# Two thirds of each feed-forward output projection as seven block products in place of eight

## The reference, cut to what matters

```python
def half_swiglu(x, g, w_in, w_out):
    a, b = jnp.split(rms_norm(x, g) @ w_in, 2, axis=-1)
    return x + 0.5 * ((jax.nn.silu(a) * b) @ w_out)
```

## Time and profile before

| | us |
|---|---|
| median of 3 runs (2575.33 to 2577.39) | 2577.12 |
| span of the profiled execution, first to last instruction | 2573.1 |
| TensorE busy in it | 2505.8 |
| VectorE / ScalarE / GpSimd busy in it | 1650.9 / 1284.6 / 805.2 |

### The profile page before, as it was taken

One profiled execution on the slowest core, in us unless ns is written; L12 is line 12 of the kernel. 1 busy time (PEld: TensorE's weight loads), 2 busy tenths in 40 slices (PEclk: granted clock), 3 DMA queues, 4 the chain that ended last, 5 costly groups with the idle time before them and its releaser, 6 DMA issues.

```text
span 2573.1 us, 48280 instructions
## 1 busy us (share of the span) xinstructions
PE 2505.8 (97%) x19339; PEld 2434.2 (95%) x19339; DVE 1650.9 (64%) x2629; ACT 1284.6 (50%) x2161; POOL 805.2 (31%) x618
## 2 busy tenths in 40 slices
PE   8999999899999989999999999999999997999998
PEld 8999999799999979999999999999998986999998
DVE  8733856888888878743766852864345548871764
ACT  7633742455555557643755742753233327661652
POOL 2232233444444442232232233233222221223222
PEclk9999999899999999999999999999999999999999
DMA  7734632133333326644635743643434333653652
GB/s 201 170 107 119 166 97 86 51 102 101 101 101 101 101 71 166 160 118 116 159 109 139 167 123 105 167 117 134 151 101 135 121 104 89 158 143 102 152 137 78
DMA packets 93305, 316.70 MB, mean 123 GB/s; under 512 B 12288, under 2 KB 16000, under 8 KB 78784
## 3 DMA queue, kind: packets, MB, share of 16 engines
q1 hardware_dynamic: 53952, 242.78, 27.8%
q0 software_dynamic: 39168, 71.32, 16.5%
HBM read 223.44 MB, written 19.32 MB: 94 GB/s over the span
## 4 chain that ended last, share of the span: by engine, by line
PE 92%; DVE 4%; DMA 2%; ACT 1%; issue 1%; POOL 0%; SPq 0%; DVEq 0%; ACTq 0%; POOLq 0%
PE ps L1415 11%; PE ps L1423 11%; PE ps L1417 11%; PE ps L1440 7%; PE ps L1441 7%; PE ps L1447 7%; PE ps L1343 7%; PE ps L1344 6%; PE ps L1349 6%; PE ps L1724 1%; DMA sb_lw<-sb_rawf 1%; PE ps L1725 1%; PE ps L1726 1%; PE ps L1388 1%; PE ps L1380 1%; PE ps L1381 1%
## 5 line engine op out<-in xcount | busy, mean ns | idle before, releaser
L1417 PE MATMUL ps<-sb_ual,sb_hw 128*128 128x288 f32 x2240 | 617.4, 296 | 0.0
L1415 PE MATMUL ps<-sb_uah,sb_hw 128*128 128x288 f32 x2240 | 615.3, 298 | 0.0
L686 POOL DMA_DIRECT2D sb_lw<-sb_rawf x240 | 207.1, 864 | 710.2 <-ACT sb_lw L850 691.1
L1415 PEld LDWEIGHTS ps<-sb_uah,sb_hw 128*128 128x128 f32 x2240 | 423.1, 189 | 0.2 <-issue 0.2
L1417 PEld LDWEIGHTS ps<-sb_ual,sb_hw 128*128 128x128 f32 x2240 | 421.6, 188 | 0.0
L662 POOL TENSOR_TENSOR sb_wl<-sb_raw,sb_wh 128x1024 fp32r<-128x1024 f32 (+1 forms) x106 | 261.1, 2466 | 433.7 <-ACT sb_wh L813 416.9
L1423 PE MATMUL ps<-sb_uah,sb_lw 128*128 128x288 f32 x2240 | 389.0, 296 | 6.1 <-DMA sb_lw<-sb_rawf 6.1
L1343 PE MATMUL ps<-sb_uh,sb_wh 128*128 128x256 f32 (+1 forms) x1360 | 373.9, 303 | 6.6 <-DVE sb_zs L2338 3.2
L1441 PE MATMUL ps<-sb_hl,sb_hw 128*128 128x288 f32 x1388 | 374.0, 296 | 0.0
L1440 PE MATMUL ps<-sb_hh,sb_hw 128*128 128x288 f32 x1388 | 373.7, 297 | 0.0
L1344 PE MATMUL ps<-sb_ul,sb_wh 128*128 128x256 f32 (+1 forms) x1360 | 368.1, 297 | 0.0
(11 more groups left out here) (319 smaller groups left out, 4785.0 us busy)
## 6 DMA issues: line engine op xcount, KB each, us to landing
sb_rawf<-w_ffn_in SPq DMA_DIRECT2D x87, 1024.0 KB, 5.0
sb_lw<-sb_rawf POOLq DMA_DIRECT2D x272, 256.0 KB, 3.7
sb_raw<-w_ssd SPq DMA_DIRECT2D x64, 512.0 KB, 3.7
sb_rawf<-w_ffn_out SPq DMA_DIRECT2D x32, 768.0 KB, 4.2
sb_rawf<-w_ffn_out SPq DMA_DIRECT2D x32, 640.0 KB, 3.9
sb_raw<-w_att SPq DMA_DIRECT2D x40, 512.0 KB, 3.6
sb_h<-state SPq DMA_DIRECT2D x8, 1024.0 KB, 4.9
ssm_sample<-sb_h SPq DMA_DIRECT2D x8, 1024.0 KB, 4.7
```

Source lines behind the costliest of these rows:

```text
L686: pool.dma_start(slot(lw, p), rawf[:, s % 2, i * BL:(i + 1) * BL], accum_op=ALU.add).then_inc(ld_in[i], 16)
L1415: pe.matmul(out, w[:, k * P:(k + 1) * P], uah[:, SIDE[p], k, :], start=begins and k == 0, stop=False, skip_group_check=True)
L1417: pe.matmul(out, w[:, k * P:(k + 1) * P], ual[:, SIDE[p], k, :], start=False, stop=False, skip_group_check=True)
```

## The change

The units of an FFN are numbered anew, 30 in place of 22 inner tiles with two rounds of eight outputs. After inner tiles 0 to 7 (units 0 to 7) come four output units over these eight tiles: unit 8 is plain and does output tiles 0 and 1 (`plain_out`, two parts); units 9, 10 and 11 do the pairs of output tiles (2,3), (4,5) and (6,7) by the seven products of `times`, now with h as the activation side. Tiles 8 to 15 and units 20 to 23 do the same again. Tiles 16 to 21 (units 24 to 29) then go through eight plain units `out(f, m)` as before, but 6 tiles deep (KO); the first two of these are interleaved in `first_outs`.

For the seven products h needs sums over pairs of inner tiles and token halves. VectorE makes them (`h_side3`, `h_sides`, `h_side4`), ScalarE their high parts (`high_hs`, `high_h4`), VectorE their low parts (`low_hs`, `low_h4`). The results of the products are added to x one by one by VectorE (`add_product`, 288 tokens each) as they stand in PSUM, since the later products go on accumulating in the same bank; TensorE waits on the semaphore x_part for that. The weights of these units are loaded as 1 MB blocks from a new array w_ffn_so, and handled as those of an inner tile. `gate` and `up` no longer exist: gr and hr, seven slots of 288 for each of four pairs of tiles, lie at the addresses of hh and hl, and all is made in place; pc keeps one slot. So `low_h` of a tile comes one unit later than before in the first 16 tiles, after the side sums that read hr. Weights of the outputs that remain use three regions of hw and lw in place of two. The distance of silu and hidden to the products of their tile, and the scaling of gate and up by rms, are as before.

The new order and the new functions (other engines' waits, semaphore names, addresses and the host's layout of the weights are left out):

```diff
+FIRST, SECOND = "first", "second"
+FULL = 2
+PLAIN_OUT = (8, 20)
+PLAIN = (0, 1) + PLAIN_OUT
+FAST_OUT = (9, 10, 11, 21, 22, 23)
+INNER = tuple(i for i in range(NU) if i not in PLAIN_OUT + FAST_OUT)
+FAST = tuple(i for i in range(NU) if i not in PLAIN)
+LAST_PART = 24
...
+REGION = (0, 1, 2, 0, 1, 2, 0, 2)
+KO = 6
...
+        for i in range(NU):
+            u = f * NU + i
+            if i < FULL:
+                yield from ((u, FIRST), (u, SECOND))
+            elif i in PLAIN_OUT:
+                yield from ((u - 1, 4), (u, FIRST), (u, SECOND))
+            elif i == FULL:
+                yield from ((u, p) for p in (1, 5, 6, 2, 3, 7))
+            elif i - 1 in PLAIN_OUT:
+                yield from ((u, p) for p in (1, 2, 5, 6, 3, 7))
+            else:
+                yield from ((u, 1), (u, 5), (u - 1, 4), (u, 6), (u, 2), (u, 3), (u, 7))
+        yield u, 4
...
+            def plain_out(s):
+                f, n, q = s // NU, s % NU, nth_full(s)
+                c = PLAIN_OUT.index(n)
+                before = nth_tile(s - 1)
+                def highs(part, ms):
+                    b = bank_full(s, part)
+                    for m in ms:
+                        if m < 2:
+                            pe.wait_ge(hp_done, 4 * q + 2 * part + m + 1)
+                        at = place(s, 2 * part + m % 2) + m // 2 * P
+                        w = hw[:, at:at + P]
+                        for h, a in enumerate(PARTS[part][m % 2][1:]):
+                            pe.matmul(ps[:, b + h, 0:HALF], w, hh[:, m // 2, a, :], start=m == 0, stop=False)
+                            pe.matmul(ps[:, b + h, 0:HALF], w, hl[:, m // 2, a, :], start=False, stop=False)
+                def lows(part, ms):
+                    b = bank_full(s, part)
+                    for m in ms:
+                        if m < 2:
+                            pe.wait_ge(lp_in[2 * part + m], 16 * (q + 1))
+                        at = place(s, 2 * part + m % 2) + m // 2 * P
+                        w = lw[:, at:at + P]
+                        for h, a in enumerate(PARTS[part][m % 2][1:]):
+                            ins = pe.matmul(ps[:, b + h, 0:HALF], w, hh[:, m // 2, a, :], start=False, stop=m == KD - 1)
+                pe.wait_ge(gate_scaled, nth_tile(s - 2) + 1)
+                pe.wait_ge(h0_free, 2 * nth_in(s - 2) + 2)
+                pe.wait_ge(h_ready, before - 1)
+                highs(0, range(4))
+                times(s - 1, 4)
+                highs(0, range(4, 6))
+                lows(0, range(6))
+                pe.wait_ge(h0_free, 2 * nth_in(s - 1 if c == 0 else s - 2) + 1)
+                highs(1, range(6))
+                lows(1, range(6))
+                pe.wait_ge(h_ready, before + 1)
+                for part in range(2):
+                    highs(part, range(6, KD))
+                    lows(part, range(6, KD)).then_inc(prod_done, 1)
...
+            def first_outs(f):
+                u, s = U_FFN[f], f * NU + NU - 1
+                before = nth_tile(s)
+                pe.wait_ge(gate_scaled, before)
+                pe.wait_ge(h0_free, 2 * nth_in(s))
+                pe.wait_ge(h_ready, before - 3)
+                pe.wait_ge(wh_done, u + 1)
+                out_highs(f, 0, range(2))
+                times(s, 4)
+                pe.wait_ge(h_ready, before)
+                out_highs(f, 0, range(2, 5))
+                pe.wait_ge(wl_done, u + 1)
+                out_lows(f, 0, range(5))
+                pe.wait_ge(h0_free, 2 * nth_in(s) - 1)
+                pe.wait_ge(wh_done, u + 2)
+                out_highs(f, 1, range(5))
+                pe.wait_ge(wl_done, u + 2)
+                out_lows(f, 1, range(5))
+                pe.wait_ge(h_ready, before + 1)
+                for m in range(2):
+                    out_highs(f, m, range(5, KO))
+                    out_lows(f, m, range(5, KO)).then_inc(unit_done, 1)
...
+            def add_direct(s, p):
+                i = BLOCK[p]
+                pool.wait_ge(nd_done, nth_direct(s, p))
+                pool.dma_start(slot(lw, p), rawf[:, s % 2, i * BL:(i + 1) * BL], accum_op=ALU.add).then_inc(ld_in[i], 16)
...
+                for n in range(NU):
+                    s = f * NU + n
+                    if n < FULL:
+                        for i in range(4):
+                            add_full(s, i)
+                    elif n in PLAIN_OUT:
+                        add_full(s, 0)
+                        add_full(s, 1)
+                        add_full(s, 2)
+                        add_direct(s + 1, 1)
+                        add_full(s, 3)
+                    elif n - 1 in PLAIN_OUT:
...
+            def high_hs(f, c, j):
+                act.wait_ge(hs_made, 3 * nth_pair(f, c, j) + 3)
+                nc.scalar.copy(hh[:, j, S1:S4, :], hr[:, j, S1:S4, :]).then_inc(hs_high, 1)
+            def high_h4(f, c):
+                act.wait_ge(h4_made, nth_pair(f, c, 3) + 1)
+                act.wait_ge(prod_done, DONE[f * NU + PLAIN_OUT[c], SECOND])
+                nc.scalar.copy(hh[:, :, S4, :], s4r[:, :, :]).then_inc(hs_high, 1)
...
+            def plain_out(s):
+                f, c = s // NU, PLAIN_OUT.index(s % NU)
+                high_full(s, 2)
+                direct(s + 1, 1)
+                high_full(s, 3)
+                silu(s - 1)
+                high_h(s - 1)
+                direct(s + 1, 2)
+                direct(s + 1, 3)
+                high_hs(f, c, 3)
+                high12(s + 1)
+            def fast_out(s):
+                f, n = s // NU, s % NU
+                if n - 1 in PLAIN_OUT:
+                    high_h4(f, PLAIN_OUT.index(n - 1))
+                    high34(s)
+                    direct(s + 1, 1)
+                    direct(s + 1, 2)
+                    high12(s + 1)
+                    direct(s + 1, 3)
+                else:
+                    direct(s + 1, 1)
+                    high34(s)
+                    high12(s + 1)
+                    direct(s + 1, 2)
+                    direct(s + 1, 3)
...
+            def h_side3(f, c, j):
+                dve.wait_ge(h_made, TILES * f + 8 * c + 2 * j + 1)
+                V.tensor_tensor(hr[:, j, S3, :], hr[:, j, A21, :], hr[:, j, A11, :], ALU.subtract).then_inc(hs_made, 1)
+            def h_sides(f, c, j):
+                dve.wait_ge(h_made, TILES * f + 8 * c + 2 * j + 2)
+                dve.wait_ge(hs_made, 3 * nth_pair(f, c, j) + 1)
+                V.tensor_tensor(hr[:, j, S2, :], hr[:, j, A22, :], hr[:, j, S3, :], ALU.add).then_inc(hs_made, 1)
+                V.tensor_tensor(hr[:, j, S1, :], hr[:, j, A22, :], hr[:, j, A21, :], ALU.add).then_inc(hs_made, 1)
+            def h_side4(f, c, j):
+                dve.wait_ge(hs_made, 3 * nth_pair(f, c, j) + 2)
+                V.tensor_tensor(s4r[:, j, :], hr[:, j, A12, :], hr[:, j, S2, :], ALU.subtract).then_inc(h4_made, 1)
+            def low_hs(f, c, j):
+                dve.wait_ge(hs_high, nth_side(f, c, j) + 1)
+                dve.wait_ge(h4_made, nth_pair(f, c, j) + 1)
+                V.tensor_tensor(hl[:, j, S1:S4, :], hr[:, j, S1:S4, :], hh[:, j, S1:S4, :].bitcast(F32),
+                                ALU.subtract).then_inc(hs_ready, 1)
+            def low_h4(f, c):
+                dve.wait_ge(hs_high, nth_side(f, c, 4) + 1)
+                V.tensor_tensor(hl[:, :, S4, :], s4r[:, :, :], hh[:, :, S4, :].bitcast(F32), ALU.subtract).then_inc(hs_ready, 1)
+            def add_plain(s, part):
+                f, b = s // NU, bank_full(s, part)
+                key = (FIRST, SECOND)[part]
+                dve.wait_ge(prod_done, DONE[s, key])
+                if s % NU != PLAIN_OUT[0]:
+                    dve.wait_ge(x_part, UPDATED[s - PLAIN_OUT[1] + PLAIN_OUT[0], key])
+                V.scalar_tensor_tensor(two(x[:, part, :]), ps[:, b:b + 2, 0:HALF], 0.5, two(x[:, part, :]),
+                                       ALU.mult, ALU.add).then_inc(x_part, 1)
+            def add_product(s, p):
+                f, n, a = s // NU, s % NU, bank_a(s)
+                m, half = ((pair_tiles(s)[0], 0) if p in (1, 2) else (pair_tiles(s)[0], 1) if p == 4
+                           else (pair_tiles(s)[1], 0) if p in (6, 3) else (pair_tiles(s)[1], 1))
+                earlier = {2: 1, 3: 6, 7: 5}
+                dve.wait_ge(prod_done, DONE[s, p])
+                if p in earlier:
+                    dve.wait_ge(x_part, UPDATED[s, earlier[p]])
+                elif n > PLAIN_OUT[1]:
+                    dve.wait_ge(x_part, UPDATED[s - PLAIN_OUT[1] + PLAIN_OUT[0], {1: 2, 5: 7, 6: 3, 4: 4}[p]])
+                t0, w = HALVES[half]
+                bank = a + {2: 2, 3: 1, 5: 1}.get(p, 0)
+                V.scalar_tensor_tensor(x[:, m, t0:t0 + w], ps[:, bank, 0:w], 0.5, x[:, m, t0:t0 + w],
+                                       ALU.mult, ALU.add).then_inc(x_part, 1)
+                s = f * NU
...
+                    if n in (5, 7, 17, 19):
+                        low_hs(f, c, int(n in (7, 19)))
```

(67 more changed lines are left out.)

892 lines of the change are left out of this document (487 added, 405 removed).

## The result

The changed kernel takes **2542.24 us** (median; 2540.4 to 2547.8), the kernel before 2577.26 beside it: ratio 0.9868, 95% interval 0.9853 to 0.9883. Predicted were 2545.0, 2538 to 2560.

What follows compares the result with a forecast made beforehand. TensorE was taken as the bound, an FFN lasting as long as its matmuls. Terms: -38.3 + 1 + 3.5 + 1.5 + 0.3 = -32.0 us, so 2577.1 becomes 2545.1; range 2538 to 2560.

Steps and rivals of the forecast that it cites:

- Matmuls: All four FFNs: 984 output matmuls each in place of 1056, 288 fewer at 0.133 us, 38.3 us gained.
- VectorE in inner tiles: Inner tiles: VectorE's added sums and low parts of h fit its 1.82 us wait per tile; cost zero.
- Fast units: Fast output units: VectorE's seven adds and the low parts come in time; cost zero, thinnest cover 0.5 us.
- Rival 3: Fast output units: products wait for in-order adds to leave their bank; decides from 1.6 us per unit, up to 2596; chance 0.04.
- Plain units: Plain output units: block 3's transfer may land late, 0 to 2.5 us for each of 8; taken 0.1 each, 1 us.
- FFN 1 to 2: Handover from FFN 1 to FFN 2: TensorE waits for late block copies and the last block; 3.5 us, bounds 0 and 6.
- FFN 2 to attention: End of FFN 2: output 7's add 0 to 3 us late, next projection has no slack; 1.5 us.
- The end: Last output: second token half has 18 matmuls, not 30, to cover the first half's norm; 0.3 us, bounds 0 and 1.6.
- Rival 4: Products with h as moving side don't come at 133 ns; 2016 matmuls x 5 ns, 10 us, giving 2555; chance 0.04.

Runs made afterwards that it cites:

- count_back: Changed kernel with 288 matmuls put back as repeats, 12 in each of the 24 fast output units: 2572.43 us (0.998).
- before_less: Kernel before with 288 low-weight output matmuls left out and nothing else changed: 2536.64 us (0.9838).
- probe_large: Changed kernel with an unneeded VectorE reciprocal, about 1.25 us, ahead of product 6's add in 16 steady fast output units: 2556.5 us (0.9927).
- load_later: Changed kernel with SP's 1 MB load three tiles behind a plain output tile held until product 1's transfer of the tile before landed: 2533.56 us (0.9838).
- blocks_first: Changed kernel with ScalarE's first three `high_full` copies moved ahead of the wait for output 6 at FFN 1's end: 2540.25 us (0.9862).

## Why the prediction was right

The time and the order of its terms are as predicted. That it came so close is partly luck: terms that it didn't have cancel.

- **Matmuls, 38.3 us.** 288 fewer, as counted. The price of 133.3 ns lies between the 111 of count_back and the 142 of before_less; with the change in long distances set against them these are 124 to 130 and 133.
- **VectorE in inner tiles, zero.** Right: no wait of TensorE names `low12` or `low34`, and VectorE still waits 1.08 and 0.69 us in the pair of tiles where it waited 1.82.
- **Fast units, zero with 0.5 us of cover.** Right; the cover is 0.40, by probe_large. Rival 3 has its mechanism shown there and its condition absent.
- **Plain units, 1 us for late transfers.** The step that was mis-sized, and mis-placed. The plain units waited 0.7. The transfers that came late are mostly those of product 1, a unit or two later, 3.5 us in five places, which load_later removes: 4.3 in all for the 1 predicted. The median of 3.7 us was taken as the landing time of any transfer, with 7.3 as a rare case; the text never laid SP's 1 MB loads beside these transfers, and where they fall together the landing is 7.1 to 9.6.
- **FFN 1 to 2, 3.5 us.** 2.3. The order was as told (output 7's add 1.8 late for 2.2; copies behind output 6; 1.29 for 1.3). The second block cost 0.25 for 0.6 and the last transfer 0.73 for 1 to 2: bounds 0 to 6 held it.
- **FFN 2 to attention, 1.5.** 1.0: 0.5 at the projection (L1494), by a low part as told, and 0.5 before that, at L1662, where output 3 waits for output 1's add to x. That the adds would hold an output unit wasn't foreseen; this one stands behind low parts that take 3.27 us in place of 1.37 beside GpSimd's subtraction. **The end, 0.3.** 0.3: 1.48 at L1738 where 1.19 stood.
- **Left out: the distance between matmuls.** The earlier trace rows was read as the price of any matmul. It was one of three, and behind the new output units the inner tiles run at 131.7; the mean distance fell by 0.8 ns, which gave back 9.8 us. Against that stand 9.2 us of long distances where 6.3 were predicted, and 4.7 in the mixers. Without the 9.8 the time would have been about 2552, inside the range but 7 us above the sum. Rival 4 had asked the right question, with the other sign.

The Trainium skill (TensorE: Matmul & The Clock Gate, Back-to-back issue gap) has 122.5 ns here by its formula for an isolated matmul; the runs show 131.7, 133.3 and 136.1, all above it. For a stream of matmuls with their weight loads it gives figures at 128 and 512 columns only, and one for each. The saving by the formula, 35.3 us, is an estimate.

Open: what selects the distance behind the output units, and what sets it at an FFN's start.

## What to carry to other kernels

Where products end faster, lay every transfer that they need beside the large loads that the other queue issues in the same microseconds: the median landing time, 3.7 us here, says nothing of those that collide, 7.1 to 9.6. One wait on the loading queue took away all 3.5 us of waits that the change had brought, and a second one 3.2 us that were there before; the times fell by more, 6.7 and 5 us, of which the rest isn't explained by waits. Work that is moved ahead must fit the idle time that it moves into: in blocks_first 3.1 us of copies went into 1.79, and one wait was exchanged for another. And take the price of a matmul from several stretches, not one, before a difference of one per cent is explained by what was changed.

## What the runs showed of the hardware that was not expected

- Transfers of two queues that are issued within 0.5 us of each other slow both: 256 KB added by GpSimd's queue took 7.1 to 9.6 us in nine profiles (8.8 in the changed kernel's) in place of 3.3, and the 1 MB load 6.2 to 8.9 (7.7) in place of 4.8.
- Matmuls of 288 columns, each with a weight load of its own, come at 131.7, 133.3 or 136.1 ns, at a granted clock of 1.00, for tens to hundreds of microseconds on end, and moving the instruction stream by one matmul left most tiles at the value that they had (58 of 80 at 133.3 both times; 59 and 69 at 131.7).
